# Attention on one Trainium2 core: the second head's softmax normalisation on GpSimd, with the delta masks queued behind it unit by unit

## The chip, the cores and the metric

One core of a Trainium2 chip runs the whole program. Five engines work side by side: TensorE (matrix products and transposes; PE in the profile, its weight loads PEld), VectorE (DVE), ScalarE (ACT), GpSimd (POOL) and SyncE (SP, which here issues the transfers). Each has its own queue of instructions, and they wait for one another through semaphores only. The metric is device time in microseconds (us), the median of several runs.

## The reference

The program is one layer of a hybrid encoder on 1024 + 512 tokens of width 1024, in float32. The part at issue is the neighbourhood attention: 8 heads of 64, tokens on a grid 64 wide, and for each block of 16 columns and 8 rows of queries the keys of some rows of 32 columns.

```python
s = jnp.einsum("bjqhd,bijkhd->bhjqik", q_r, k_r).astype(jnp.float32)
bias = rpb[:, dr_idx[None, None, :, None], dc_idx[:, :, None, :]]
s = jnp.where(col_ok[:, :, None, :], s + bias, -jnp.inf)
p = jax.nn.softmax(s.reshape(s.shape[:4] + (kh * NA_KB,)), axis=-1).reshape(s.shape)
return jnp.einsum("bhjqik,bijkhd->bjqhd", p.astype(v.dtype), v_r)
```

After it comes a gated delta rule in chunks (`_delta_rule_chunked`). It needs decay matrices `exp(g_i - g_j)` that are cut to the lower (or, for the backward direction, upper) triangle, with and without the diagonal, and a triangular solve, which the kernel does by joining blocks of doubling size.

## The kernel before

The program is a row of stages with a barrier of all engines between them: projection, attention, delta rule, merge, MLP. The change lies in `attention` (L994 to L1263) and its helper `delta_masks` (L1266 to L1293).

`attention` goes over 48 units `u`: 4 pairs of heads, in each 3 groups of 8 rows, in each 4 column blocks. A unit is two heads of 128 queries against 384 keys (units 0 to 7 of a pair) or 256 keys (units 8 to 11); this number is its width. Its two heads are `h = 0` and `h = 1`. A unit goes through these steps, each an instruction or a few, and the steps of neighbouring units overlap:

- TensorE multiplies queries by keys into `ps_s` (L1129, the score). Two scores may be ahead.
- VectorE adds the bias, negates, takes the row minimum (L1186, into `sc` and `nmax`), once per head.
- ScalarE takes the exponential with the row sum (L1243, into `pr` and `rsum`), once per head.
- VectorE inverts both sums (L1193, `rinv`) and multiplies each head by its column of them (L1198, `pn`, the normalisation).
- TensorE transposes `pn` of both heads into `ps_t` (L1171, the turn of the heads).
- ScalarE copies that to `pt` (L1253), TensorE multiplies by the values into `ps_o` (L1158, the mix), VectorE copies the result out (L1220).

In the first 8 units of a pair TensorE also transposes values (L1141, the value turn), which VectorE copies (L1206). All loops are written out by hand: in iteration `u` TensorE's order is score of `u + 1`, mix of `u - 2`, value turn of `u`, turn of the heads of `u - 1`. VectorE's is bias of `u`, reciprocal and normalisation of `u - 1`, value copy of `u`, output copy of `u - 2`. ScalarE's is exponentials of `u`, copies of `u - 1`, then one or two exponentials of the delta rule's decay (L1233). `sc`, `pr`, `pn` and `pt` hold two units each.

Work for the delta rule is done in this stage beside the attention. GpSimd alone makes the masks: `strict` and `incl` (8 instructions) and then `join`, seven levels of ten small instructions each, all in one chain (`delta_masks`), and after them twelve additions of a mask to the decay rows `gq` (L1109, 128 x 512, into `dd0`). VectorE does eight small instructions on decay columns (`decay_columns`, L978 to L985) in iteration 6. SyncE's queue issues the loads of queries, keys, values, bias tables and decay rows. `join` is read in the stage after.

Of the kernel before, what the change touches and what calls it, by code (L numbers as in the profile page):

```python
# [18 lines left out]
ALU = mybir.AluOpType  # L19
AX = mybir.AxisListType  # L20

P = 128
# [5 lines left out]
TB = 512  # L28
NTB = T // TB
# [10 lines left out]
NEG = -1e30  # L40

HEADS = 4
LEVELS = 7
# [950 lines left out]
def attention(nc, proj, v_mid, bias_t, o_t, ident, masks, dn_y, g_rows, cols, ahead, oz):  # L994

    U = NH_PAIR * NA_UNITS
# [22 lines left out]
    strict, incl, join = masks  # L1019
    y2, gq, kb, col2, ncol2, cx2 = ahead  # L1020
    dd0 = kb[:].rearrange("p (a j) n -> p a j n", j=4)
    DG_AT, DCOL_AT, DY_AT, DEXP_AT = 1, 6, (28, 32, 36), 8
    DEXP = 2 * 2 * NTB * 4

    with Space(nc, "na") as s:
        dg_in, dy_in, d_cols, d_colexp, d_masked, d_exp, d_chain = (s.sem(x) for x in (
            "dg_in", "dy_in", "d_cols", "d_colexp", "d_masked", "d_exp", "d_chain"))
        q_in, k_in, v_in = ([[s.sem(f"{x}{a}{b}") for b in range(2)] for a in range(2)] for x in ("q_in", "k_in", "v_in"))
        bias_in = [s.sem(f"bias_in{b}") for b in range(NBB)]
        stored = [s.sem(f"stored{b}") for b in range(2)]  # L1030
        scored, biased, exped, recip, normed, turned, copied, mixed, out_done, v_turned, v_copied, seen = (s.sem(x) for x in (
            "scored", "biased", "exped", "recip", "normed", "turned", "copied", "mixed", "out_done", "v_turned", "v_copied",
            "seen"))
        mask_chain, mask_work = s.sem("mask_chain"), s.sb("mask_work", [P])
        qt, kt, vt = s.sb("qt", [2, T]), s.sb("kt", [2, T]), s.sb("vt", [2, 2, 2, T // 2])
# [65 lines left out]

        @block.gpsimd
        def _(pool):
            delta_masks(pool, mask_chain, mask_work, *masks)
            pool.wait_ge(dg_in, 32)
            for n in range(2 * NTB):
                tg, d = divmod(n, 2)
                for q, mask in enumerate((strict, incl)):
                    pool.tensor_tensor(dd0[:, 2 * n + q], gq[:, 0, d, tg * TB:(tg + 1) * TB].rearrange("p (j n) -> p j n", n=P),  # L1109
                                       mask[:, d].unsqueeze(1).to_broadcast([P, 4, P]), ALU.add).then_inc(d_masked, 1)  # L1110

        @block.tensor
        def _(pe):
            def score(u):
                i, g, j, k0, n, width = unit(u)
                if g == 0:
                    if j == 0:
                        pe.wait_ge(q_in[0][i % 2], 16 * (i // 2) + 16)
                        pe.wait_ge(k_in[0][i % 2], 16 * (i // 2) + 16)
                elif j == 0 and g == 1:  # L1120
                    pe.wait_ge(q_in[1][i % 2], 16 * (i // 2) + 16)
                    pe.wait_ge(k_in[1][i % 2], 16 * (i // 2) + 16)
                if u >= 2:
                    pe.wait_ge(biased, 2 * u - 2)
                keys = kt[:, i % 2].rearrange("p (r c) -> p r c", c=GRID)
                q = qt[:, i % 2, (g * NA_BLOCKS + j) * P:(g * NA_BLOCKS + j + 1) * P]
                for h in range(2):
                    r = slice(64 * h, 64 * h + 64)
                    last = pe.matmul(ps_s[:, u % 2, h, 0:width].rearrange("p (r c) -> p r c", c=NA_COLS), q[r],  # L1129
                                     keys[r, k0:k0 + n, na_col0(j):na_col0(j) + NA_COLS], start=True, stop=True,  # L1130
                                     tile_position=(64 * h, 0))
                last.then_inc(scored, 1)

            def turn_values(u):
                i, k = group(u)
                j, rest = k % NA_BLOCKS, k // NA_BLOCKS
                pe.wait_ge(v_in[rest][i % 2], 32 * (i // 2) + 32)
                v = vt[:, i % 2, j % 3 != 0, j // 2]
                for t in range(3):
                    at = (3 * rest + t) * P  # L1140
                    last = pe.transpose(ps_o[:, u % 2, (t + 1) * P:(t + 2) * P], v[:, at:at + P], ident[:])  # L1141
                last.then_inc(v_turned, 1)
            score(0)
            for u in range(U + 2):
                if u + 1 < U:
                    score(u + 1)
                m = u - 2
                if m >= 0:
                    i, g, j, k0, n, width = unit(m)
                    pe.wait_ge(copied, 2 * m + 2)  # L1150
                    pe.wait_ge(v_copied, groups_to(m))
                    if m >= 2:
                        pe.wait_ge(out_done, m - 1)
                    tiles = width // P
                    for t in range(tiles):
                        for h in range(2):
                            r = slice(64 * h, 64 * h + 64)
                            last = pe.matmul(ps_o[r, m % 2, 0:P], vtm[:, j, k0 // 4 + t, r], pt[:, m % 2 * 2 + h, t * P:(t + 1) * P],  # L1158
                                             start=(t == 0), stop=(t == tiles - 1), tile_position=(0, 64 * h))
                    last.then_inc(mixed, 1)  # L1160
                if group(u) is not None:
                    turn_values(u)
                m = u - 1
                if 0 <= m < U:
                    width = unit(m)[-1]
                    for h in range(2):
                        pe.wait_ge(normed, 2 * m + h + 1)
                        if m:
                            pe.wait_ge(copied, 2 * (m - 1) + h + 1)
                        for t in range(width // P):  # L1170
                            last = pe.transpose(ps_t[:, h, t * P:(t + 1) * P], pn[:, m % 2 * 2 + h, t * P:(t + 1) * P], ident[:])  # L1171
                        last.then_inc(turned, 1)

        @block.vector
        def _(dve):
            for u in range(U + 2):
# [13 lines left out]
                if 0 <= m < U:  # L1190
                    width = unit(m)[-1]
                    dve.wait_ge(exped, 2 * m + 2)
                    dve.reciprocal(rinv[:, 2 * m:2 * m + 2], rsum[:, 2 * m:2 * m + 2]).then_inc(recip, 1)  # L1193
                    dve.wait_ge(recip, m + 1)
                    for h in range(2):
                        if m >= 2:
                            dve.wait_ge(turned, 2 * (m - 2) + h + 1)
                        dve.tensor_scalar(pn[:, m % 2 * 2 + h, 0:width], pr[:, m % 2 * 2 + h, 0:width],  # L1198
                                          rinv[:, 2 * m + h:2 * m + h + 1], None, ALU.mult).then_inc(normed, 1)
                if group(u) is not None:  # L1200
                    i, k = group(u)
                    j, rest = k % NA_BLOCKS, k // NA_BLOCKS
# [22 lines left out]
        def _(act):  # L1225
# [10 lines left out]
            for u in range(U + 1):  # L1236
                if u < U:
                    width = unit(u)[-1]
                    for h in range(2):
                        act.wait_ge(biased, 2 * u + h + 1)  # L1240
                        if u >= 2:
                            act.wait_ge(normed, 2 * (u - 2) + h + 1)
                        act.activation(pr[:, u % 2 * 2 + h, 0:width], sc[:, u % 2 * 2 + h, 0:width], ACT.Exp,  # L1243
                                       bias=nmax[:, 2 * u + h:2 * u + h + 1], scale=-1.0,
                                       accum_out=rsum[:, 2 * u + h:2 * u + h + 1]).then_inc(exped, 1)
# [17 lines left out]
            act.wait_ge(d_colexp, 1)  # L1263


def delta_masks(pool, chain, work, strict, incl, join):  # L1266

    def keep(n, tile, pattern, base, step, fill=0.0):

        pool.wait_ge(chain, n)  # L1270
        pool.affine_select(out=tile, in_=tile, compare_op=ALU.is_ge, fill=fill, base=base, pattern=pattern,
                           channel_multiplier=step).then_inc(chain, 1)

    n = 0
    for tile, fill, col, row, base in ((strict[:, 0], -NEG, -1, 1, -1), (strict[:, 1], -NEG, 1, -1, -1),
                                       (incl[:, 0], NEG, 1, -1, 0), (incl[:, 1], NEG, -1, 1, 0)):
        pool.memset(tile, 0.0).then_inc(chain, 1)
        keep(n + 1, tile, [[col, P]], base, row, fill)
        n += 2
    for v in range(LEVELS):  # L1280
        m = 2 ** v
        for d in range(2):

            blocks = work[:].rearrange("p (c two m) -> p c two m", two=2, m=m)[:, :, 1 - d]
            pool.wait_ge(chain, n)
            pool.memset(work[:], 0.0).then_inc(chain, 1)
            pool.wait_ge(chain, n + 1)
            pool.memset(blocks, 1.0).then_inc(chain, 1)
            keep(n + 2, blocks, [[-2 * m, P // (2 * m)], [0, m]], -d * m, 1)
            keep(n + 3, blocks, [[2 * m, P // (2 * m)], [0, m]], m - 1 + d * m, -1)  # L1290
            pool.wait_ge(chain, n + 4)
            pool.tensor_copy(join[:, v, d], work[:]).then_inc(chain, 1)
            n += 5  # L1293
    pool.wait_ge(chain, n)


DCHAINS = [(d, g) for g in range(len(SEG)) for d in range(2)]
# [1274 lines left out]
```

## Time and profile before

| | |
|---|---|
| median of 3 runs | 3128.47 us (3127.68 to 3128.94) |
| the profiled execution | 3127.74 us, its span 3126.0 us |
| mean granted clock of TensorE | 0.983 |
| busy in the span | PE 2993.6 us (96%), DVE 1334.8 (43%), ACT 1152.9 (37%), POOL 1184.4 (38%) |
| attention stage, 1100 to 1252 us | PE 128.3 us busy, DVE 116.6, ACT 106.8, POOL 36.7; clock 0.91 |
| L1198 in it | 96 instructions, 36.5 us |
| L1109 in it | 12 instructions of about 1.3 us |

The times are those of one profiled execution, counted from the start of its span. An instruction's time includes what it waits for once its engine has begun it. In brackets stands how long the engine was idle before an instruction, and which instruction, by the semaphores, ended that. PEclk is the share of full speed (2.4 GHz) that TensorE was granted; 0.50 is 1.2 GHz. The timeline merges neighbouring instructions of one kind: x2 is two of them, and the time is from the start of the first to the end of the last.

### The profile page before, as it was taken

To read this page: it belongs to the slowest core of one execution; us is meant where nothing else is said; L and a number is where in the kernel's file an instruction comes from. 1 tells how busy PE (TensorE), PEld (TensorE's weight loads), DVE (VectorE), ACT (ScalarE), POOL (GpSimd) and SP (SyncE) were. 2 spreads that over 40 slices of the span, in tenths; PEclk is the share of its full clock that TensorE was granted. 3 is DMA by queue.
4 is the path that set the end of the run, shared out by engine and by line. 5 is a ranking of instruction groups with operands and counts; after the bars stand their busy time and mean duration, and the time that the engine had idled before them with its cause. 6 is when DMAs were issued, how large, how long until landed. Compare 5 with 4: busy or idle time off the path is not lost. (4 is left out here: it accounts for less than half of the span.)

```text
span 3126.0 us, 44278 instructions
## 1 busy us (share of the span) xinstructions
PE 2993.6 (96%) x17907; PEld 2451.2 (78%) x17907; DVE 1334.8 (43%) x1933; ACT 1152.9 (37%) x1932; POOL 1184.4 (38%) x777
## 2 busy tenths in 40 slices
PE   5999999999999969899998999979999999999998
PEld 4878787877888746788887887868888888888887
DVE  4233232312379968667664353122224232322323
ACT  4241413243144548566664122232232323333222
POOL 4221121212123240123200433456665666666764
PEclk8999999999999989999999999989999999999999
DMA  4434232433545375111103545332333233333331
GB/s 112 164 137 131 75 117 83 134 102 118 164 143 175 112 245 185 64 53 56 39 22 112 175 148 170 95 125 91 108 92 97 89 100 122 94 95 95 109 114 61
DMA packets 239594, 353.15 MB, mean 113 GB/s; under 512 B 32928, under 2 KB 186272, under 8 KB 239392
## 3 DMA queue, kind: packets, MB, share of 16 engines
q1 hardware_dynamic: 239392, 350.32, 34.6%
q8 instruction: 144, 2.36, 0.3%
q14 instruction: 58, 0.48, 0.0%
HBM read 263.71 MB, written 96.36 MB: 115 GB/s over the span
## 5 line engine op out<-in xcount | busy, mean ns | idle before, releaser
L102 PE MATMUL pj_acc<-u_hi,pj_w_hi 128*128 128x512 f32 x1464 | 576.2, 394 | 13.0 <-POOL u_lo L543 13.0
L2484 DVE TENSOR_TENSOR x_tm<-m_ps,x_tm 128x512 f32<-128x512 f32 x384 | 265.0, 691 | 744.1 <-PE m_ps L104 744.1
L104 PE MATMUL pj_acc<-u_hi,pj_w_lo 128*128 128x512 f32 x1464 | 571.7, 390 | 0.0
L103 PE MATMUL pj_acc<-u_lo,pj_w_hi 128*128 128x512 f32 x1464 | 571.2, 390 | 0.0
L537 POOL TENSOR_TENSOR pj_w_lo<-pj_w_raw,pj_w_hi 128x1024 fp32r<-128x1024 f32 x61 | 157.8, 2586 | 729.7 <-ACT pj_w_hi L586 729.7
L102 PEld LDWEIGHTS pj_acc<-u_hi,pj_w_hi 128*128 128x128 f32 x1464 | 275.7, 188 | 88.0 <-issue 18.2
L2361 POOL TENSOR_TENSOR m_w_lo<-m_w_raw,m_w_hi 128x1024 fp32r<-128x1024 f32 x96 | 237.8, 2501 | 263.0 <-ACT m_w_hi L2275 263.0
L104 PEld LDWEIGHTS pj_acc<-u_hi,pj_w_lo 128*128 128x128 f32 x1464 | 275.7, 188 | 58.2
L103 PEld LDWEIGHTS pj_acc<-u_lo,pj_w_hi 128*128 128x128 f32 x1464 | 275.9, 188 | 56.4
L102 PE MATMUL m_ps<-m_v_hi,m_w_hi 128*128 128x512 f32 x768 | 299.6, 390 | 2.4 <-DVE m_v_lo L2452 2.4
L102 PE MATMUL m_ps<-m_w_hi,m_h_hi 128*128 128x512 f32 x768 | 299.6, 390 | 0.0
L104 PE MATMUL m_ps<-m_v_hi,m_w_lo 128*128 128x512 f32 x768 | 299.3, 390 | 0.0
L103 PE MATMUL m_ps<-m_v_lo,m_w_hi 128*128 128x512 f32 x768 | 299.2, 390 | 0.0
L104 PE MATMUL m_ps<-m_w_hi,m_h_lo 128*128 128x512 f32 x768 | 298.9, 389 | 0.0
L103 PE MATMUL m_ps<-m_w_lo,m_h_hi 128*128 128x512 f32 x768 | 298.8, 389 | 0.0
L2354 POOL TENSOR_TENSOR m_w_lo<-m_w_raw,m_w_hi 128x1024 fp32r<-128x1024 f32 x96 | 227.8, 2395 | 22.7 <-ACT m_w_hi L2268 22.7
L2060 POOL TENSOR_TENSOR mo_w_lo<-mo_w_raw,mo_w_hi 128x512 fp32r<-128x512 f32 x72 | 94.2, 1308 | 307.1 <-ACT mo_w_hi L2022 307.1
L586 ACT CAST pj_w_hi<-pj_w_raw 128x1024 fp32r<-128x1024 f32 x61 | 63.8, 1046 | 375.8 <-PE pj_acc L104 375.2
L2287 ACT CAST m_h_hi<-m_rel 128x512 fp32r<-128x512 f32 x96 | 59.6, 621 | 357.7 <-POOL m_rel L2367 357.7
L2275 ACT CAST m_w_hi<-m_w_raw 128x1024 fp32r<-128x1024 f32 x96 | 96.1, 1050 | 247.6 <-PE m_ps L104 247.6
L102 PEld LDWEIGHTS m_ps<-m_v_hi,m_w_hi 128*128 128x128 f32 x768 | 144.6, 188 | 32.8 <-DVE m_v_lo L2452 2.8
L104 PEld LDWEIGHTS m_ps<-m_v_hi,m_w_lo 128*128 128x128 f32 x768 | 144.5, 188 | 30.1
(283 smaller groups left out, 5278.7 us busy)
## 6 DMA issues: line engine op xcount, KB each, us to landing
m_w_raw<-in_w_mlp_dram SPq DMA_DIRECT2D x48, 1024.0 KB, 5.4
m_w_raw<-in_w_mlp_dram SPq DMA_DIRECT2D x96, 512.0 KB, 3.6
proj<-pj_stage SPq DMA_DIRECT2D x61, 768.0 KB, 3.5
pj_w_raw<-in_w_in_dram SPq DMA_DIRECT2D x61, 512.0 KB, 5.1
mo_gate<-proj SPq DMA_DIRECT2D x24, 768.0 KB, 4.4
mo_w_raw<-in_w_out_dram SPq DMA_DIRECT2D x48, 256.0 KB, 2.6
rpb_bias<-pj_shut SPq DMA_DIRECT2D x48, 192.0 KB, 3.0
rpb_bias<-rpb_near SPq DMA_DIRECT2D x24, 384.0 KB
```

The lines of the kernel that those rows point to most:

```text
L102: pe.matmul(out, w_hi, x_hi, start=first, stop=False)
L103: pe.matmul(out, w_hi, x_lo, start=False, stop=False)
L104: return pe.matmul(out, w_lo, x_hi, start=False, stop=last)
L537: pool.tensor_tensor(w_lo[:, n % 2], w_raw[:, n % 2], w_hi[:, n % 2].bitcast(F32), ALU.subtract).then_inc(lo_done, 1)
L586: act.copy(w_hi[:, n % 2], w_raw[:, n % 2]).then_inc(hi_done, 1)
L2060: pool.tensor_tensor(w_lo[:, sl % 2], w_raw[:, sl % 3], w_hi[:, sl % 2].bitcast(F32), ALU.subtract).then_inc(w_lo_done, 1)
L2275: act.copy(w2_hi[:, (2 * gg + j) % 4], w2_raw[:, j]).then_inc(w2_hi_done, 1)
L2287: act.copy(h_hi[:, m % 4], rel[:, j]).then_inc(hh_done, 1)
L2354: pool.tensor_tensor(w1_lo[:, m % 4], w1_raw[:, :, j * P:(j + 1) * P], w1_hi[:, m % 4].bitcast(F32), ALU.subtract).then_inc(w1_lo_done, 1)
L2361: pool.tensor_tensor(w2_lo[:, m % 4], w2_raw[:, j], w2_hi[:, m % 4].bitcast(F32), ALU.subtract).then_inc(w2_lo_done, 1)
L2484: dve.tensor_tensor(xt, ps2[:, q % 4], xt, ALU.add).then_inc(added, 1)
```

## The change

The multiply of head 1 goes from VectorE to GpSimd, with a semaphore `normed_b` of its own; TensorE's turn of head 1 and ScalarE's reuse of `pr` wait for it. GpSimd's queue is rearranged: first only `strict` and `incl`, then for each unit the multiply, behind which stands one addition of L1109 in units 5 to 16 and one level of `join` in units 20 to 26.

```diff
@@ GpSimd's queue in attention
-            delta_masks(pool, mask_chain, mask_work, *masks)
-            pool.wait_ge(dg_in, 32)
-            for n in range(2 * NTB):
+            def normal(m):
+                width = unit(m)[-1]
+                pool.wait_ge(recip, m + 1)
+                if m >= 2:
+                    pool.wait_ge(turned, 2 * (m - 2) + 2)
+                pool.tensor_scalar(pn[:, m % 2 * 2 + 1, 0:width], pr[:, m % 2 * 2 + 1, 0:width],
+                                   rinv[:, 2 * m + 1:2 * m + 2], None, ALU.mult).then_inc(normed_b, 1)
+            def masked(a):
+                n, q = divmod(a, 2)
                 tg, d = divmod(n, 2)
-                for q, mask in enumerate((strict, incl)):
-                    pool.tensor_tensor(dd0[:, 2 * n + q], gq[:, 0, d, tg * TB:(tg + 1) * TB].rearrange("p (j n) -> p j n", n=P),
-                                       mask[:, d].unsqueeze(1).to_broadcast([P, 4, P]), ALU.add).then_inc(d_masked, 1)
+                if a == 0:
+                    pool.wait_ge(dg_in, 32)
+                pool.tensor_tensor(dd0[:, a], gq[:, 0, d, tg * TB:(tg + 1) * TB].rearrange("p (j n) -> p j n", n=P),
+                                   (strict, incl)[q][:, d].unsqueeze(1).to_broadcast([P, 4, P]), ALU.add).then_inc(d_masked, 1)
+            delta_masks(pool, mask_chain, mask_work, *masks, 0)
+            for m in range(U):
+                normal(m)
+                a = m - DEXP_AT + 3
+                if 0 <= a < 2 * 2 * NTB:
+                    masked(a)
+                v = m - DEXP_AT - 2 * 2 * NTB
+                if 0 <= v < LEVELS:
+                    delta_masks(pool, mask_chain, mask_work, *masks, v + 1)
@@ TensorE
-                        pe.wait_ge(normed, 2 * m + h + 1)
+                        pe.wait_ge((normed, normed_b)[h], m + 1)
@@ VectorE
-                    for h in range(2):
-                        if m >= 2:
-                            dve.wait_ge(turned, 2 * (m - 2) + h + 1)
-                        dve.tensor_scalar(pn[:, m % 2 * 2 + h, 0:width], pr[:, m % 2 * 2 + h, 0:width],
-                                          rinv[:, 2 * m + h:2 * m + h + 1], None, ALU.mult).then_inc(normed, 1)
+                    if m >= 2:
+                        dve.wait_ge(turned, 2 * (m - 2) + 1)
+                    dve.tensor_scalar(pn[:, m % 2 * 2, 0:width], pr[:, m % 2 * 2, 0:width],
+                                      rinv[:, 2 * m:2 * m + 1], None, ALU.mult).then_inc(normed, 1)
@@ ScalarE
-                            act.wait_ge(normed, 2 * (u - 2) + h + 1)
+                            act.wait_ge((normed, normed_b)[h], u - 1)
@@ delta_masks: part 0 makes strict and incl, part v + 1 makes level v of join
-def delta_masks(pool, chain, work, strict, incl, join):
+def delta_masks(pool, chain, work, strict, incl, join, part):
```

Here `DEXP_AT` is 8, `NTB` 3, `LEVELS` 7 and `U` 48.

## Rows read from the trace of the kernel before

**Rows 1.** busy time in one 10 us stretch; after the time: busy us (instructions) per engine, PEclk, DMA

```profile
1170.00:1180.00 10.00, 10.00 (x96) 6.94 (x94) 9.36 (x37) 9.06 (x29) 0.00 (x0) 1.00 0.52 160
```

**Rows 2.** timeline of all engines, one 384-wide unit; columns: start us, us, engine, line

```profile
1167.02 0.92 PE L1129 MATMUL na_ps_s<-na_kt,na_qt 64*128 64x384 f32 x4
...
1167.87 0.88 PE L1158 MATMUL na_ps_o<-na_pt,na_vtm 128*64 128x128 f32 x12
...
1168.10 0.16 DVE L1193 RECIPROCAL na_rinv<-na_rsum 128x2 f32<-128x2 f32 x1
...
1168.29 0.75 DVE L1198 TENSOR_SCALAR na_pn<-na_pr,na_rinv 128x384 f32<-128x384 f32 x2
...
1168.67 0.55 PE L1141 MATMUL na_ps_o<-ident,na_vt 128*128 128x128 f32 x3
...
1169.06 0.82 PE L1171 MATMUL na_ps_t<-ident,na_pn 128*128 128x128 f32 x6
1169.26 0.56 DVE L1206 COPY na_vtm<-na_ps_o 128x384 f32<-128x384 f32 x1 [0.22 <-PE na_ps_o L1141]
...
1169.81 0.92 PE L1129 MATMUL na_ps_s<-na_kt,na_qt 64*128 64x384 f32 x4
```

**Rows 3.** timeline of the tensor engine, one 256-wide unit

```profile
1182.39 0.70 PE L1129 MATMUL na_ps_s<-na_kt,na_qt 64*128 64x256 f32 x4
...
1183.61 0.42 PEld L1171 LDWEIGHTS na_ps_t<-ident,na_pn 128*128 128x128 f32 x4 [0.17 <-DVE na_pn L1198]
...
1184.20 0.92 PE L1129 MATMUL na_ps_s<-na_kt,na_qt 64*128 64x384 f32 x4
```

**Rows 4.** timeline of VectorE and GpSimd, units 5 to 7

```profile
1128.59 1.26 POOL L1109 TENSOR_TENSOR dn_kb<-dn_gq,strict 128x512 f32<-128x512 f32 x1 [1.65 <-DMA dn_gq<-g_rows]
...
1130.86 1.77 DVE L1198 TENSOR_SCALAR na_pn<-na_pr,na_rinv 128x384 f32<-128x384 f32 x2
...
1131.03 1.39 POOL L1109 TENSOR_TENSOR dn_kb<-dn_gq,strict 128x512 f32<-128x512 f32 x1
...
1134.36 2.19 DVE L1198 TENSOR_SCALAR na_pn<-na_pr,na_rinv 128x384 f32<-128x384 f32 x2
...
1136.95 0.78 DVE L978 COPY dn_col<-cols 128x48 f32<-128x48 f32 x1
...
1142.85 0.29 DVE L1220 COPY oz<-na_ps_o 128x128 f32<-128x128 f32 x1
```

**Rows 5.** timeline of VectorE in the stage after, the same small instructions alone

```profile
1316.51 0.17 DVE L978 COPY dn_col<-cols 128x48 f32<-128x48 f32 x1
...
1317.21 0.16 DVE L985 COPY dn_cx<-dn_gq 128x12 f32<-128x12 f32 x1
```

**Rows 6.** timeline of VectorE, L1198 for units 6, 11, 30 and 35

```profile
1144.30 0.75 DVE L1198 TENSOR_SCALAR na_pn<-na_pr,na_rinv 128x384 f32<-128x384 f32 x2
...
1157.29 0.62 DVE L1198 TENSOR_SCALAR na_pn<-na_pr,na_rinv 128x256 f32<-128x256 f32 x2
...
1206.53 0.75 DVE L1198 TENSOR_SCALAR na_pn<-na_pr,na_rinv 128x384 f32<-128x384 f32 x2
...
1217.13 0.61 DVE L1198 TENSOR_SCALAR na_pn<-na_pr,na_rinv 128x256 f32<-128x256 f32 x2
```

**Rows 7.** busy time in a 2 us stretch, columns as in Rows 1

```profile
1146.00:1148.00 2.00, 2.00 (x12) 1.10 (x12) 1.22 (x7) 1.66 (x6) 0.00 (x0) 0.50 1.01 309
```

**Rows 8.** timeline of GpSimd: first and last instruction of the seven mask levels, a copy

```profile
1102.93 0.21 POOL L1286 MEMSET na_mask_work<- 128x128 f32 x1
...
1126.62 0.31 POOL L1292 CAST join<-na_mask_work 128x128 uint8<-128x128 f32 x1
...
1252.43 3.40 POOL L1425 COPY dn_tn<-ident 128x512 f32<-128x512 f32 x6 [108.60 <-POOLq L78]
```

**Rows 9.** timeline of VectorE, L1198 for units 20 and 27

```profile
1180.78 0.62 DVE L1198 TENSOR_SCALAR na_pn<-na_pr,na_rinv 128x256 f32<-128x256 f32 x2
...
1198.17 0.75 DVE L1198 TENSOR_SCALAR na_pn<-na_pr,na_rinv 128x384 f32<-128x384 f32 x2
```

More of the change, by code:

```diff
@@ L1030, in attention @@
         stored = [s.sem(f"stored{b}") for b in range(2)]
-        scored, biased, exped, recip, normed, turned, copied, mixed, out_done, v_turned, v_copied, seen = (s.sem(x) for x in (
-            "scored", "biased", "exped", "recip", "normed", "turned", "copied", "mixed", "out_done", "v_turned", "v_copied",
+        scored, biased, exped, recip, normed, normed_b, turned, copied, mixed, out_done, v_turned, v_copied, seen = (s.sem(x) for x in (
+            "scored", "biased", "exped", "recip", "normed", "normed_b", "turned", "copied", "mixed", "out_done", "v_turned", "v_copied",
             "seen"))
@@ L1272, in keep @@
                            channel_multiplier=step).then_inc(chain, 1)
[L1274 to L1293, printed above, removed]
+    if part == 0:
+        n = 0
+        for tile, fill, col, row, base in ((strict[:, 0], -NEG, -1, 1, -1), (strict[:, 1], -NEG, 1, -1, -1),
+                                           (incl[:, 0], NEG, 1, -1, 0), (incl[:, 1], NEG, -1, 1, 0)):
+            pool.memset(tile, 0.0).then_inc(chain, 1)
+            keep(n + 1, tile, [[col, P]], base, row, fill)
+            n += 2
+        pool.wait_ge(chain, n)
+        return
+    v = part - 1
+    n = 8 + 10 * v
+    m = 2 ** v
+    for d in range(2):
+        blocks = work[:].rearrange("p (c two m) -> p c two m", two=2, m=m)[:, :, 1 - d]
+        pool.wait_ge(chain, n)
+        pool.memset(work[:], 0.0).then_inc(chain, 1)
+        pool.wait_ge(chain, n + 1)
+        pool.memset(blocks, 1.0).then_inc(chain, 1)
+        keep(n + 2, blocks, [[-2 * m, P // (2 * m)], [0, m]], -d * m, 1)
+        keep(n + 3, blocks, [[2 * m, P // (2 * m)], [0, m]], m - 1 + d * m, -1)
+        pool.wait_ge(chain, n + 4)
+        pool.tensor_copy(join[:, v, d], work[:]).then_inc(chain, 1)
+        n += 5
     pool.wait_ge(chain, n)
```

## The prediction

> **What bounds the kernel now.** The table of the page comes first: TensorE carries the end of the whole program, VectorE is busy 43% of it and GpSimd 38%. The change touches one stage of some 150 us, so I read that stage alone. Its busy times in a settled stretch [rows 1] show three engines that all look full: TensorE 10.00 of 10, VectorE 9.36, ScalarE 9.06. GpSimd does nothing. The question is which of the three sets the pace, and the timeline of one unit answers it [rows 2]. TensorE takes four pieces in a fixed order: score 1167.02 to 1167.87 (0.85), mix to 1168.67 (0.80), value turn to 1169.06 (0.39), turn of the two heads to 1169.81 (0.75). Together that is 2.79 us, the whole period, with no piece late. VectorE has a wait in the same unit: 0.22 us in front of L1206, for TensorE's value turn. So TensorE paces, and VectorE, though 94% busy, is the one that waits. A unit of width 256 has the same shape [rows 3]: 1184.20 - 1182.39 = 1.81 us from score to score, and the turn begins after a wait of 0.17 us on L1198, short enough to be TensorE's ordinary cost of a wait. Time taken off VectorE is therefore worth nothing while the stage runs undisturbed.
>
> **Where it is disturbed.** Around units 5 to 7 GpSimd runs its twelve mask additions (L1109, 1.26 us each) back to back [rows 4]. VectorE's two normalisations of a unit then take 1.77 and 2.19 us where they take 0.75 [rows 2], and eight small instructions (L978 to L985), which in the next stage need 1317.21 + 0.16 - 1316.51 = 0.86 us [rows 5], stretch here from 1136.95 to about 1142.7 [rows 4]. VectorE and GpSimd take turns: each VectorE instruction waits for a whole addition. TensorE gets nothing for some 5 us, and its granted clock falls to 0.50 [rows 7], the 1.2 GHz level. From unit 6 to unit 11 the stage then takes 1157.29 - 1144.30 = 12.99 us, against 1217.13 - 1206.53 = 10.60 us for the same units two pairs later [rows 6].
>
> **Part 1: the second head's multiply.** 48 instructions leave VectorE, about 0.31 to 0.38 us each (half of 0.62 and 0.75). In the settled units that is worth 0, by the argument above; the cover is TensorE, and if TensorE were not the pace it would be up to 0.35 us a unit. What counts is when the second head is ready. Before, that is 0.04 + 0.75 = 0.79 us after the reciprocal ends (1168.26 to 1169.04) [rows 2]. TensorE starts that head's three turns about 0.3 us after it starts the first head's (a little under half of the 0.75 us), so hardly before 1169.25: a margin of 0.2 us. After, GpSimd sees the reciprocal about 0.10 us late (my estimate; VectorE itself needs 0.03), finds VectorE's first-head multiply under way, and multiplies. No GpSimd multiply by a column is in the trace. Bounds for 384 wide: a GpSimd copy of 512 columns takes 3.40 / 6 = 0.57 us [rows 8], so by width 0.43; an addition of two tensors of 512 takes 1.26 [rows 4], so by width 0.95. It has one tensor input like the copy, and a multiply more: I take 0.55 (0.42 at 256, bounds 0.28 and 0.63). For the meeting with VectorE: the addition that began 0.17 us after a multiply of VectorE took 1.39 instead of 1.26 [rows 4], 0.13 more. Ready at 0.10 + 0.13 + 0.55 = 0.78 us, the same as before. Cost 0; above 0.75 us for the multiply it begins to cost.
>
> The Trainium skill, SBUF — State Buffer, section "Who interferes with whom", says of the port pair that VectorE and GpSimd share that the one who comes second "fully blocks" for the other's whole instruction. By that rule the second head would be ready at 0.04 + 0.38 + 0.55, about 1.0 us, which just uses up the margin. The trace bears out the blocking where the addition comes first (1.77 and 2.19 us [rows 4]), but shows only 0.13 us where the multiply comes first.
>
> **Part 2: the additions spread out.** One addition follows the multiply of each of units 5 to 16. The first stall loses 1.77 - 0.75 = 1.0 us and the second 2.19 - 0.75 = 1.4 us; following TensorE's order through them, of these 2.4 us some 2.0 reach L1206 of unit 6. The eight small instructions meet the tail of one addition instead of five of them: about 0.3 + 0.9 + 0.4 us in place of the 5.9 us from 1136.95 to 1142.85 [rows 4], 4.3 us less. TensorE is then idle for under 2 us, so I expect the clock to stay up, and units 6 to 11 to take 10.6 us and not 13.0: 2.4 us. Gain 2.0 + 4.3 + 2.4 = 8.7 us; 6.3 if the clock falls all the same. Against it, behind the 256-wide units 8 to 11 GpSimd needs 0.23 + 0.42 + 1.26, about 1.9 us, in a period of 1.81: 0.5 us lost in all.
>
> **Part 3: the mask levels, which I think are what decides.** Before, the seven levels (70 small instructions) run from 1102.93 to 1126.93, 24.0 us [rows 8], while nobody waits for GpSimd. After, level v stands behind the multiply of unit 20 + v, and the multiply of the next unit stands behind the level. A level takes 24.0 / 7 = 3.4 us on average, but units come every 1.8 to 2.8 us. So from unit 20 to 27 GpSimd is the pace, and it never waits: reciprocal of unit 20 at 1180.75 [rows 9], + 0.23 + 0.42 for its multiply, + 24.0 of levels, + 3 x 0.42 + 3 x 0.55 for units 21 to 26, + 7 x 0.10 between them, + 0.55 for unit 27: 1209.6. Before, unit 27 is ready at 1198.17 + 0.75 = 1198.9 [rows 9], with 0.2 us in hand. So 10.5 us are lost. The double buffers hide none of it, for TensorE can't turn the second head of a unit before GpSimd has written it, and L1158 of that unit and L1220 wait behind. TensorE will have gaps of 1 to 3 us in these units; I add 0.5 for its clock.
>
> **The sum.** -8.7 + 0.5 + 10.5 + 0.5 = +2.8 us. The profiled execution took 3127.74 us (its span 3126.0), so 3130.5; the median of the runs lies 0.73 us above that execution: 3131.3 us.
>
> **Rivals.**
> - *The multiply costs as much as an addition* (0.95 and 0.63 us), or takes the port first. In the mask stretch that adds 4 x 0.4 + 4 x 0.21 = 2.4 us. In some 28 other units of width 384 the second head is late by about 0.2, of which half to all reaches the period: about 4 us. Total +9.2: 3137.7. For it: every GpSimd row with two tensors is slow. Against: this multiply has one.
> - *The clock falls in the mask stretch.* TensorE works 1.8 us in every 4 to 5. If it enters the 384-wide units 24 to 26 at 0.50, each takes over 5 us where GpSimd needs 3.6. Up to 3 x 1.5 = 4.5 us more: 3135.8. For it: the fall in [rows 7]. Against: that one followed 5 us of complete idleness.
> - *VectorE is the pace after all, and the kernel gets faster.* Then each of the 41 units outside the stretch gains about 0.35 us, 14 us: 3131.3 - 14 = 3117. It decides if the period of a 384-wide unit falls below 2.6 us. For it: 9.36 of 10 busy. Against: the wait of 0.22 us in every such unit.
> - *The change does little of this:* the levels' delay is partly taken up by work done ahead (one unit of 2.8 us at most), giving 3128.5.
>
> **How the numbers follow.** Forecast as summed 0.50; multiply or port dearer 0.17; clock 0.15; VectorE the pace 0.10; levels partly absorbed 0.08. The likeliest case's own range is 3126 to 3134. 0.2% is 6.3 us, about what a measurement of this kernel can tell from no change: below 3122.2 counts as faster, above 3134.7 as slower. Faster: the VectorE rival and a little of the forecast's low end, 0.12. Slower: the first two rivals less a part that falls short, 0.28. The same: 0.60. The range of 3122 to 3138 leaves out the VectorE rival and the high ends of the others.
>
> **What would show it.** L1198's row on VectorE halves to 48 with no instruction of 1.7 us or more. The gap in front of L1206 in settled units grows from 0.22 to about 0.6 at a period of 2.79: right; a period of 2.4: the VectorE rival. The eight small instructions end within 2 us. The new GpSimd multiply's mean shows 0.55 or 0.95. Between units 20 and 27 GpSimd is busy without a break and TensorE's longest waits name it; if the starts of L1198 for units 20 and 27 are about 28 us apart instead of 17.4, part 3 is right. The prediction fails if the levels delay nobody (then faster by 8 us) or the clock drops for most of the stretch.

## The result, and the profile after

The changed kernel takes 3142.45 us (median of 5 runs, 3141.49 to 3146.05) against 3128.94 us (5 runs, 3127.68 to 3130.84) of the kernel before, measured together: a ratio of 1.0046, 95% interval 1.0035 to 1.0058. It is slower by 13.5 us. The forecast was 3131.3 with a range of 3122 to 3138, and no change within 0.2% as the likeliest outcome. Neither holds: the measured time lies beyond the dear end of the range.

The profiled execution (span 3142.4) loses it all in the attention stage. From GpSimd's first instruction there to its first in the next stage the stage took 1252.43 - 1100.44 = 151.99 us before and 1269.49 - 1101.15 = 168.34 us after, 16.35 us more; everything else takes the same 2974 us.

The first view is that of the groups of instructions, in the stage of the changed kernel. Behind the bar stand busy us and mean ns of one, and then the idle time before.

```profile
L1110 POOL TENSOR_SCALAR na_pn<-na_pr,na_rinv 128x384 f32<-128x384 f32 x32 | 45.8, 1431 | 49.8 <-DVE na_rinv L1212 49.3
...
L1110 POOL TENSOR_SCALAR na_pn<-na_pr,na_rinv 128x256 f32<-128x256 f32 x16 | 16.7, 1044 | 10.6 <-DVE na_rinv L1212 10.2
...
L1119 POOL TENSOR_TENSOR dn_kb<-dn_gq,strict 128x512 f32<-128x512 f32 x6 | 7.6, 1266 | 0.0
...
L1216 DVE TENSOR_SCALAR na_pn<-na_pr,na_rinv 128x384 f32<-128x384 f32 x32 | 14.3, 448 | 1.1
```

L1110 is GpSimd's multiply: 1431 ns at 384 columns, 1044 ns at 256. The estimate was 550 and 420, its upper bounds 950 and 630. The addition next to it, with two tensors and 512 columns, takes 1266. So here a GpSimd instruction with one tensor and a column takes longer for 384 columns than one with two tensors for 512.

A settled stretch, all engines, to be held against [rows 2] (units 40 and 41):

```profile
1246.12 0.16 DVE L1212 RECIPROCAL na_rinv<-na_rsum 128x2 f32<-128x2 f32 x1
1246.32 0.42 DVE L1216 TENSOR_SCALAR na_pn<-na_pr,na_rinv 128x384 f32<-128x384 f32 x1
1246.38 1.47 POOL L1110 TENSOR_SCALAR na_pn<-na_pr,na_rinv 128x384 f32<-128x384 f32 x1 [1.86 <-DVE na_rinv L1212]
...
1247.29 0.56 DVE L1224 COPY na_vtm<-na_ps_o 128x384 f32<-128x384 f32 x1 [0.55 <-PE na_ps_o L1160]
...
1247.90 0.31 PEld L1190 LDWEIGHTS na_ps_t<-ident,na_pn 128*128 128x128 f32 x3 [0.56 <-POOL na_pn L1110]
...
1249.11 0.42 DVE L1216 TENSOR_SCALAR na_pn<-na_pr,na_rinv 128x384 f32<-128x384 f32 x1
...
1250.61 0.56 DVE L1224 COPY na_vtm<-na_ps_o 128x384 f32<-128x384 f32 x1 [1.09 <-PE na_ps_o L1160]
...
1252.43 0.42 DVE L1216 TENSOR_SCALAR na_pn<-na_pr,na_rinv 128x384 f32<-128x384 f32 x1
```

GpSimd begins 0.06 us after VectorE and is done at 1246.38 + 1.47 = 1247.85; TensorE, which had turned the first head, waits 0.56 us for that and goes on at 1247.90. VectorE's multiplies start at 1246.32, 1249.11 and 1252.43: periods of 2.79 and 3.32 us alternate, 3.06 on average where [rows 2] had 2.79. VectorE's wait before L1224 (the L1206 of before) is 0.55 and 1.09 us where it was 0.22. So VectorE did get free, and waits longer.

The waits of TensorE on GpSimd's multiply in the whole stage, with total us, count and the longest:

```profile
PEld na_ps_t L1190 <- POOL na_pn L1110: 21.1, 26, 3.3
...
PE na_ps_t L1190 <- POOL na_pn L1110: 14.6, 21, 3.1
```

None of these existed before. The mask levels, in GpSimd's timeline:

```profile
1179.04 1.08 POOL L1110 TENSOR_SCALAR na_pn<-na_pr,na_rinv 128x256 f32<-128x256 f32 x1 [0.94 <-DVE na_rinv L1212]
1180.07 0.20 POOL L1308 MEMSET na_mask_work<- 128x128 f32 x1
...
1184.28 0.29 POOL L1314 CAST join<-na_mask_work 128x128 uint8<-128x128 f32 x1
1184.67 0.93 POOL L1110 TENSOR_SCALAR na_pn<-na_pr,na_rinv 128x256 f32<-128x256 f32 x1
1185.54 0.20 POOL L1308 MEMSET na_mask_work<- 128x128 f32 x1
...
1197.72 1.25 POOL L1110 TENSOR_SCALAR na_pn<-na_pr,na_rinv 128x384 f32<-128x384 f32 x1
...
1210.02 0.29 POOL L1314 CAST join<-na_mask_work 128x128 uint8<-128x128 f32 x1
1210.41 1.25 POOL L1110 TENSOR_SCALAR na_pn<-na_pr,na_rinv 128x384 f32<-128x384 f32 x1
```

To be held against [rows 8, 9]: unit 20's multiply begins at 1179.04, level 0 stands behind it until 1184.57, and only then comes unit 21's multiply, although its reciprocal has long been there. GpSimd has no idle time until unit 27's multiply at 1210.41. From unit 20 to unit 27 it is 31.4 us by these starts; by VectorE's own, which is ahead of GpSimd here, it is 29.0 us, against 17.4 before by those of [rows 9]. The multiplies take 0.93 and 1.25 us here, where no multiply of VectorE runs beside them: that is their price alone. VectorE's copies and biases, which read PSUM, do run beside some of them and make no difference.

VectorE in units 5 to 7, to be held against [rows 4, 5]:

```profile
1136.85 0.54 DVE L978 COPY dn_col<-cols 128x48 f32<-128x48 f32 x1
...
1137.92 0.17 DVE L985 COPY dn_cx<-dn_gq 128x12 f32<-128x12 f32 x1
...
1141.56 1.10 DVE L1216 TENSOR_SCALAR na_pn<-na_pr,na_rinv 128x384 f32<-128x384 f32 x1
```

The eight small instructions (L978 to L985) end at 1138.09, after 1.24 us, where they took 5.75. But a new blocked multiply stands at 1141.56: 1.10 us instead of 0.42, for it met an addition of GpSimd's that was under way, and GpSimd's own multiply stood behind that addition:

```profile
1141.18 1.26 POOL L1119 TENSOR_TENSOR dn_kb<-dn_gq,incl 128x512 f32<-128x512 f32 x1
...
1142.42 1.34 POOL L1110 TENSOR_SCALAR na_pn<-na_pr,na_rinv 128x384 f32<-128x384 f32 x1
```

TensorE's granted clock, in three windows (the column before the last two):

```profile
1142.00:1144.00 2.00, 2.00 (x13) 1.26 (x14) 0.66 (x1) 1.47 (x5) 2.00 (x3) 0.50 0.97 286
...
1184.00:1188.00 4.00, 2.35 (x8) 0.95 (x10) 0.00 (x0) 1.63 (x6) 3.38 (x11) 0.70 0.63 164
...
1196.00:1200.00 4.00, 3.29 (x19) 2.23 (x16) 2.20 (x8) 1.40 (x6) 3.38 (x11) 0.50 1.04 393
```

It was at 0.50 again around units 7 and 8. In the stretch of the levels it fell to 0.70 with TensorE busy for 2.35 of 4 us, and to 0.50 later on.

### The profile page after: what moved, and what is told of

It is laid out like the page before. It is cut to its first block and busy times, and to the rows that moved or that the text cites. A ratio compares the mean times of both kernels' runs of the same rounds, so it can differ in the third digit from the quotient of the medians.

```text
span 3142.4 us, 44324 instructions
## 1 busy us (share of the span) xinstructions
PE 3004.4 (96%) x17907; PEld 2453.4 (78%) x17907; DVE 1316.0 (42%) x1885; ACT 1155.3 (37%) x1932; POOL 1244.8 (40%) x825
```

## The experiments

Where the stage's time goes, by the starts of VectorE's reciprocal (L1193 of before) in each kernel's timeline: us from the stage's start to unit 6, then from unit to unit, then the whole stage up to GpSimd's first instruction of the next. What follows unit 47 is 6.5 to 6.6 us in every kernel and has no column. Each row is one profiled execution.

| kernel | to 6 | 6 to 8 | 8 to 20 | 20 to 27 | 27 to 47 | stage | median of all runs |
|---|---|---|---|---|---|---|---|
| before | 43.66 | 5.85 | 30.63 | 17.40 | 47.91 | 151.99 | 3128.94; 3128.49; 3127.14 |
| changed | 38.33 | 6.31 | 33.00 | 29.01 | 55.13 | 168.34 | 3142.45 |
| e1 both on VectorE | 36.93 | 6.18 | 36.80 | 17.51 | 47.91 | 151.86 | 3129.18 |
| e2 levels in gaps | 39.91 | 4.78 | 33.25 | 18.81 | 53.01 | 156.30 | 3131.19 |
| e4 two-tensor multiply | 38.68 | 6.20 | 32.33 | 26.52 | 53.87 | 164.15 | 3138.63 |
| e5 no second multiply | 36.31 | 5.52 | 34.65 | 17.41 | 47.90 | 148.33 | 3124.17 |
| e6 last 128 columns | 38.92 | 4.06 | 29.98 | 17.44 | 47.95 | 144.90 | 3121.20 |
| e7 additions behind multiplies | 37.47 | 4.05 | 29.92 | 17.52 | 47.91 | 143.40 | 3119.67 |
| e8 two-tensor and gaps | 37.47 | 5.34 | 33.13 | 18.89 | 52.66 | 154.04 | 3128.51 |
| e9 before, paced additions | 36.92 | 4.05 | 29.88 | 17.41 | 47.91 | 142.71 | 3116.36 |

The three medians of before are those of the three sets in which it ran beside the changed kernel, e1 to e5, and e6 to e9. In the two later sets its runs spread over 3122 to 3133 us, more than in the first. What lies outside the stage, which no edit touches, takes between 2970.5 and 2978.2 us in the ten profiled executions (span less stage), while equal pieces of the stage agree within 0.12 us (the columns 20 to 27 and 27 to 47 of before, e1, e5, e7 and e9). So the stage's length is the sharper measure of one cause, and the ratio, with its interval, that of the whole.

**e1: both multiplies on VectorE, GpSimd's other work still spread.**

```diff
@@ GpSimd: the multiply goes, the wait for each unit stays
             def normal(m):
                 pool.wait_ge(recip, m + 1)
-                if m >= 2:
-                    pool.wait_ge(turned, 2 * (m - 2) + 2)
-                pool.tensor_scalar(pn[:, m % 2 * 2 + 1, 0:width], pr[:, m % 2 * 2 + 1, 0:width],
-                                   rinv[:, 2 * m + 1:2 * m + 2], None, ALU.mult).then_inc(normed_b, 1)
@@ VectorE
+                    if m >= 2:
+                        dve.wait_ge(turned, 2 * (m - 2) + 2)
+                    dve.tensor_scalar(pn[:, m % 2 * 2 + 1, 0:width], pr[:, m % 2 * 2 + 1, 0:width],
+                                      rinv[:, 2 * m + 1:2 * m + 2], None, ALU.mult).then_inc(normed_b, 1)
```

> Both multiplies stay on VectorE; GpSimd's additions and mask levels stay spread over the units as in the change (it still waits for each unit's reciprocal). Theory A (the loss is the GpSimd multiply, dear by itself and queued behind the levels; the spreading alone is a gain): the gaps of part 2 stay closed and nobody waits for the levels, 3128.9 - 8 = about 3121 us, and L1198's successor again takes 0.75 us for two. Rival B (the spread work on GpSimd itself disturbs VectorE in every unit through what the two share): no better than before, 3129 us or more, with VectorE's multiplies longer than 0.42 us in units 5 to 16 and 20 to 26.

Ratio to before 1.0001 (0.9992 to 1.0009): neither theory whole. The stretch of the levels is back at 17.51 us and the last one at 47.91, so the levels cost nothing with no multiply behind them. The closed gap is there too (36.93 to unit 6). But from unit 8 to 20 the stage loses 6.2 us. VectorE and GpSimd in units 13 and 14:

```profile
1160.55 1.53 DVE L1211 TENSOR_SCALAR na_pn<-na_pr,na_rinv 128x384 f32<-128x384 f32 x1
1160.59 1.27 POOL L1114 TENSOR_TENSOR dn_kb<-dn_gq,strict 128x512 f32<-128x512 f32 x1 [2.32 <-DVE na_rinv L1207]
...
1162.00 0.41 DVE L1215 TENSOR_SCALAR na_pn<-na_pr,na_rinv 128x384 f32<-128x384 f32 x1
...
1164.13 1.53 DVE L1211 TENSOR_SCALAR na_pn<-na_pr,na_rinv 128x384 f32<-128x384 f32 x1
1164.18 1.27 POOL L1114 TENSOR_TENSOR dn_kb<-dn_gq,incl 128x512 f32<-128x512 f32 x1 [2.32 <-DVE na_rinv L1207]
```

VectorE's first multiply begins at 1160.55, GpSimd's addition at 1160.59, both released by the same reciprocal, and the multiply takes 1.53 us: the addition has its 1.27 us undisturbed, and the multiply ends 0.22 us after it. That is the rival's mark, an instruction of 1.5 us in place of 0.42. It belongs to this kernel, in which the additions start together with VectorE's multiply; in the changed one GpSimd's own multiply stands in front of them.

**e2: the levels in GpSimd's idle time.** `delta_masks` is cut into half levels.

```diff
-                v = m - DEXP_AT - 2 * 2 * NTB
-                if 0 <= v < LEVELS:
-                    delta_masks(pool, mask_chain, mask_work, *masks, v + 1)
+                for x in LEVEL_AT.get(m, ()):
+                    delta_masks(pool, mask_chain, mask_work, *masks, x + 1)
@@ before the loop
+            LEVEL_AT = {-1: (0, 1, 2, 3), 2: (4, 5, 6, 7), 3: (8, 9), 4: (10,), 17: (11,), 24: (12,), 28: (13,)}
+            for x in LEVEL_AT[-1]:
+                delta_masks(pool, mask_chain, mask_work, *masks, x + 1)
```

> The change, but the fourteen half levels stand where GpSimd was idle in the changed kernel: four before unit 0, four behind unit 2, two behind unit 3, one each behind units 4, 17, 24 and 28. Theory A: units 20 to 27 took 31.4 us against 17.4 before; without the levels they take about 19 (the dear multiply stays), so 3142.5 - 12 = about 3130 us. Rival C (the levels are incidental, the clock of TensorE or the multiply alone makes the loss): over 3138 us.

Ratio 1.0011 (1.0002 to 1.0020). The stage is 12.0 us shorter than in the changed kernel, 10.2 of them between units 20 and 27 and 2.1 behind. That is close to theory A's number. What is left over before from unit 8 on is 53.01 against 47.91 us in the last twenty units, 1.4 between 20 and 27, 2.6 between 8 and 20. That the first two are the multiply on GpSimd is shown by e5 below, which has the same half levels and no such multiply, and is back at 47.90 and 17.41.

**e4: GpSimd's multiply as a product of two tensors.**

```diff
-                pool.tensor_scalar(pn[:, m % 2 * 2 + 1, 0:width], pr[:, m % 2 * 2 + 1, 0:width],
-                                   rinv[:, 2 * m + 1:2 * m + 2], None, ALU.mult).then_inc(normed_b, 1)
+                pool.tensor_tensor(pn[:, m % 2 * 2 + 1, 0:width], pr[:, m % 2 * 2 + 1, 0:width],
+                                   rinv[:, 2 * m + 1:2 * m + 2].to_broadcast([P, width]), ALU.mult).then_inc(normed_b, 1)
```

> The change, with GpSimd's multiply written as a product of two tensors, the column of reciprocals spread over the width. Theory A1 (the form with a scalar column is what makes 1.25 and 0.93 us alone): 0.95 and 0.63 us alone as the prediction's upper bound had it, 0.22 more beside VectorE, and the kernel about 3136 us. Rival A2 (the price is that of a multiply or of its columns in any form): 1.25 us or more again and 3142 us.

Ratio 1.0035 (1.0022 to 1.0049), 3138.6 us: between A1's 3136 and A2's 3142. The stage is 4.2 us shorter than the changed kernel's. The groups on GpSimd, then VectorE's first multiply beside GpSimd's in a settled unit:

```profile
L1110 POOL TENSOR_TENSOR na_pn<-na_pr,na_rinv 128x384 f32<-128x384 f32 x32 | 26.6, 831 | 64.6 <-DVE na_rinv L1212 64.2
...
L1110 POOL TENSOR_TENSOR na_pn<-na_pr,na_rinv 128x256 f32<-128x256 f32 x16 | 9.9, 620 | 16.1 <-DVE na_rinv L1212 15.9
```

```profile
1235.42 1.09 DVE L1216 TENSOR_SCALAR na_pn<-na_pr,na_rinv 128x384 f32<-128x384 f32 x1
1235.46 0.83 POOL L1110 TENSOR_TENSOR na_pn<-na_pr,na_rinv 128x384 f32<-128x384 f32 x1 [2.36 <-DVE na_rinv L1212]
```

The form was the price: 831 and 620 ns for the same products, less even than A1 had put it. And yet the period is only 3.0 us instead of 3.06, because now GpSimd takes its 0.83 us undisturbed and VectorE's multiply of the first head takes 1.09 instead of 0.42: the lateness moved from head 1 to head 0.

**e5: head 1 is not normalised** (TensorE turns `pr`, and ScalarE's reuse of `pr` waits for that turn; the output lacks the division), half levels as in e2.

```diff
-                        pe.wait_ge((normed, normed_b)[h], m + 1)
+                        pe.wait_ge((normed, recip)[h], m + 1)
@@ the source of each turn
-pn[:, m % 2 * 2 + h, t * P:(t + 1) * P]
+(pn, pr)[h][:, m % 2 * 2 + h, t * P:(t + 1) * P]
```

> Head 1 is not normalised at all: TensorE turns its exponentials straight from pr. GpSimd has no multiply, its half levels stand as in the run with the levels in gaps. Theory A (TensorE is the pace of a settled unit): VectorE does 0.38 us less a unit and the period of a 384-wide unit stays 2.79 us, the kernel within 3 us of the run with both multiplies on VectorE, about 3120 us. Rival D (VectorE is the pace): 2.4 us a unit and about 3107 us.

Ratio 0.9991 (0.9981 to 1.0000). A settled unit:

```profile
1224.68 0.30 PEld L1145 LDWEIGHTS na_ps_s<-na_kt,na_qt 64*128 64x128 f32 x4 [0.17 <-issue]
...
1226.91 0.56 DVE L1221 COPY na_vtm<-na_ps_o 128x384 f32<-128x384 f32 x1 [0.55 <-PE na_ps_o L1157]
...
1227.46 0.30 PEld L1145 LDWEIGHTS na_ps_s<-na_kt,na_qt 64*128 64x128 f32 x4 [0.17 <-issue]
```

1227.46 - 1224.68 = 2.78 us from score to score, the period of [rows 2], and VectorE's wait grew from 0.22 to 0.55. With a third of a microsecond less to do in each unit, units 20 to 47 take what they took before (17.41 and 47.90 us). TensorE is the pace, and VectorE is not. The kernel's time missed the expected 3120 by 4 us. Units 8 to 20 take 34.65 us, 4.7 more than in e7 below: the additions start together with VectorE's multiply, as in e1.

**e7: as e1, each addition behind VectorE's second multiply.**

```diff
                 if a == 0:
                     pool.wait_ge(dg_in, 32)
+                pool.wait_ge(normed_b, a + DEXP_AT - 2)
```

> As the run with both multiplies on VectorE, but each addition waits for VectorE's second multiply of its unit instead of for the reciprocal. In that run units 12 to 17 had a period of 3.59 us against 2.79, with VectorE's first multiply at 1.53 us beside an addition that began 0.04 us after it. Theory A (the additions are harmless unless they start together with a multiply): the period is 2.79 again, the gain of the closed gap is kept, about 3121 us. Rival B (an addition costs VectorE its 1.1 us wherever it stands in a unit): 3128 us or more.

Ratio 0.9975 (0.9965 to 0.9986), a gain of 7.8 us by the ratio. Units 8 to 20 take 29.92 us, the period there is 2.79. The collision cost 6.9 us in e1, and the only edit is where the additions begin: about 1.1 us after the reciprocal's start where it had been 0.23.

**e9: the kernel before with nothing but that wait.**

```diff
                 for q, mask in enumerate((strict, incl)):
+                    pool.wait_ge(normed, 2 * (2 * n + q + DEXP_AT - 2))
```

> The kernel before with one wait added: each of the twelve additions on GpSimd waits for both multiplies of its unit (5 to 16). Mask levels stay where they were, at the start. Theory A: like the run before it, about 3121 us; the levels' place is of no matter as long as no multiply is queued behind them. Rival (moving the levels away from the start is part of the gain, since they disturb units 0 to 3): this one is 1 us or more slower than the other.

Ratio 0.9967 (0.9955 to 0.9980), the best kernel here: its stage is 9.28 us shorter than before, 0.69 shorter than e7's. Moving the levels was no part of the gain. VectorE and GpSimd in units 5 to 7, the stretch of [rows 4]:

```profile
1134.21 0.75 DVE L1199 TENSOR_SCALAR na_pn<-na_pr,na_rinv 128x384 f32<-128x384 f32 x2
...
1135.14 1.27 POOL L1110 TENSOR_TENSOR dn_kb<-dn_gq,strict 128x512 f32<-128x512 f32 x1 [7.15 <-DVE na_pn L1199]
...
1136.99 0.17 DVE L985 COPY dn_cx<-dn_gq 128x12 f32<-128x12 f32 x1
...
1138.74 0.75 DVE L1199 TENSOR_SCALAR na_pn<-na_pr,na_rinv 128x384 f32<-128x384 f32 x2
...
1139.57 1.28 POOL L1110 TENSOR_TENSOR dn_kb<-dn_gq,incl 128x512 f32<-128x512 f32 x1 [3.16 <-DVE na_pn L1199]
```

The eight small instructions end at 1137.16, the two multiplies take 0.75 us together again, and the additions fall between them. The clock, in the stretch that had it at 0.50:

```profile
1138.00:1142.00 4.00, 2.78 (x26) 2.04 (x27) 3.93 (x18) 3.15 (x10) 1.50 (x2) 1.00 0.51 144
1142.00:1146.00 4.00, 4.00 (x39) 2.60 (x38) 3.42 (x16) 3.89 (x14) 2.53 (x3) 1.00 0.38 118
```

It stays at 1.00.

**e8: the change with both mendings** (e4's multiply and e2's placing of the levels).

> The change with both mendings: GpSimd's multiply as a product of two tensors (0.83 us alone) and the levels in GpSimd's idle time. Theory A (two separate losses that add): 3142.5 - 11.3 (levels) - 4 (form) = about 3127 us, no better than before, because a settled 384-wide unit still takes 3.0 us instead of 2.79. Rival (once the levels are away the multiply on GpSimd pays): below 3122 us.

Ratio 1.0002 (0.9993 to 1.0011). The losses add to within 2 us (168.34 - 12.04 - 4.19 = 152.1 us for the stage, 154.04 measured), and what is left equals the gain of the spreading: a mended form of this change is worth nothing.

**e6: GpSimd multiplies only the last 128 columns of head 1**, half levels as in e2.

```diff
-                pool.tensor_scalar(pn[:, m % 2 * 2 + 1, 0:width], pr[:, m % 2 * 2 + 1, 0:width],
+                pool.tensor_scalar(pn[:, m % 2 * 2 + 1, width - P:width], pr[:, m % 2 * 2 + 1, width - P:width],
@@ VectorE, after its multiply of head 0
+                    dve.tensor_scalar(pn[:, m % 2 * 2 + 1, 0:width - P], pr[:, m % 2 * 2 + 1, 0:width - P],
+                                      rinv[:, 2 * m + 1:2 * m + 2], None, ALU.mult)
@@ TensorE, before the last of head 1's turns
+                            if h and t == width // P - 1:
+                                pe.wait_ge(normed_b, m + 1)
```

> The change with levels in the gaps, GpSimd multiplying only the last 128 columns of head 1 and VectorE the rest. From 1.25 and 0.93 us alone at 384 and 256 columns a line gives 0.61 at 128, 0.83 beside VectorE. Theory A (the period grows by how late GpSimd is beyond a margin of about 0.2 us): ready in time, 2.79 us a unit, 3123 to 3126 us in all. Rival E (a GpSimd multiply disturbs VectorE's two whatever its width): 3.0 us or more a unit and 3130 us or more.

Ratio 0.9977 (0.9966 to 0.9988), 3121.2 us by the median, a little below the expected span. One of its seven runs took 6032.95 us, which nothing here explains; the six others lie between 3117.4 and 3122.7. A settled unit:

```profile
1225.26 0.42 DVE L1220 TENSOR_SCALAR na_pn<-na_pr,na_rinv 128x384 f32<-128x384 f32 x1
1225.32 0.88 POOL L1110 TENSOR_SCALAR na_pn<-na_pr,na_rinv 128x128 f32<-128x128 f32 x1 [1.90 <-DVE na_rinv L1216]
...
1225.59 0.46 DVE L1224 TENSOR_SCALAR na_pn<-na_pr,na_rinv 128x256 f32<-128x256 f32 x1
...
1226.22 0.56 DVE L1232 COPY na_vtm<-na_ps_o 128x384 f32<-128x384 f32 x1 [0.17 <-PE na_ps_o L1162]
```

GpSimd's 128 columns take 0.88 us beside two instructions of VectorE's (the line through 1.25 and 0.93 us gives 0.61 alone, an estimate; in unit 3, where it began after both of VectorE's had ended, it took 0.60). They are ready at 1226.20, and TensorE's turn runs through without a wait: 47.95 us for units 27 to 47. As soon as GpSimd is in time, its multiply costs nothing in these units, and gains nothing either (47.91 in e7 without it).

## Why the prediction was wrong

**What bounds: right.** TensorE paces the settled units; e5 takes away VectorE's work and the period stays 2.78 to 2.79.

**Part 1, the second head's multiply: the step that failed.** The prediction priced it "0.55 (0.42 at 256, bounds 0.28 and 0.63)" and at 384 bounded it by 0.43 and 0.95, from a copy and from an addition of two tensors. It measured 1.25 and 0.93 us alone and 1.47 and 1.08 beside VectorE, outside the bounds. The bound from above rested on the thought that an instruction with one tensor can't be dearer than one with two; e4 shows the opposite (0.83 and 0.62 for two). The mechanism was laid out rightly: the prediction said that "above 0.75 us for the multiply it begins to cost", and 1.47 us makes the period 3.06. No run tests the 0.75 itself: at 0.83 us (e4) it is the first head that comes late, and e6, at 0.88 us, has only the last third of the columns to deliver. The term was 0; it measured 2.6 + 1.4 + 5.1 = 9.1 us (e2 against before, from unit 8 on). The rival "the multiply costs as much as an addition" named this loss and was too cheap as well, at a surcharge of 6.4 us over the forecast; it set the dear end of the range, 3137.7.

**Part 2, the additions spread out: the place right, the size half.** To unit 6 the changed kernel gains 5.3 us, against 6.3 in the forecast; the eight small instructions end after 1.24 us. The 2.4 us of the clock did not come: it fell around units 7 and 8, as the prediction had allowed, after TensorE had waited first 1.4 us for VectorE's multiply of unit 6 and then 0.8 us for GpSimd's. The full forecast of 8.7 us is what the additions give once they meet no multiply: 8.6 us in e7, 9.3 in e9. The 0.5 us that the prediction put on the additions behind GpSimd's multiply were no underestimate: in the changed kernel units 12 to 20, which hold five of them, take 23.12 us, and units 36 to 44, which hold none, 23.12 as well. What it had no price for is an addition released together with VectorE's multiply, which holds that up for 1.1 us (e1, 6.2 us in all); the changed kernel is spared that by the multiply in front. [Rows 4] held a relative of it: the 1.77 us end at 1132.63, 0.21 after the addition of 1131.03 does. But not "each VectorE instruction waits for a whole addition": in the same trace the copy L1206 out of PSUM took 0.54 us at 1132.56, beside an addition from 1132.38 to 1133.76.

**Part 3, the mask levels: right.** 10.5 us and 0.5 for the clock were forecast; taking the levels away (e2) gives 12.0, and e1 shows that they cost nothing with no multiply behind them. By the prediction's sum unit 27's second head is ready 1209.56 - 1180.75 = 28.81 us after unit 20's reciprocal ends; it was 1211.66 - 1178.95 = 32.71. That is 3.9 us later, and the eight multiplies in that queue were 5.0 us dearer than forecast (one at 1.08 and three at 0.93 for 0.42, four at 1.25 for 0.55), so the levels themselves were not underpriced. e4 agrees: with multiplies cheaper by 0.3 to 0.5 us each the seven units take 26.52 us instead of 29.01.

**The sum.** Stage against stage: -5.3 to unit 6, +0.5 to unit 8, +2.4, +11.6, +7.2 to unit 47, together +16.3 us. By cause: the levels 12.0 (forecast 11.0), the multiply and its meetings from unit 8 on 9.1 (0.5 in all), the spreading up to unit 8 gives back 4.8 (8.7). Of the 13.5 us by which the stage missed the forecast, 8.6 are thus Part 1, 3.9 Part 2 and 1.0 Part 3. In e9, where the spreading meets nothing, the stage is at unit 8 3.7 us sooner than in the changed kernel (40.97 against 44.64 us), although no level is in the queue yet: that is the shortfall of Part 2, the clock's share in it. The waits of units 6 and 7 speak for the late multiplies as its cause; it was not tried apart. The median moved by 13.5 us only; the stage is that of one profiled execution, which took 3144.17 us, 16.4 more than that of before (3127.74).

**The rivals.** VectorE is not the pace: in the middle of a run of 384-wide units no kernel has a period under 2.78 us. The clock did fall in the mask stretch (0.70 from 1184 to 1188, 0.50 from 1196 to 1200), but it set no pace: GpSimd has no idle time up to unit 27's multiply, and its multiplies of units 24 to 27 start (1210.41 - 1197.72) / 3 = 4.2 us apart at either clock, one level and one multiply. Whether it cost something behind unit 27 was not tried. "Levels partly absorbed" did not occur.

**The meeting of the two multiplies.** The Trainium skill, SBUF — State Buffer, section "Who interferes with whom", has whichever of the two issues first, GpSimd or a VectorE instruction in a two-port mode, hold the shared pair and the other one fully blocked. The prediction weighed it and went by a delay of 0.13 us. Where VectorE's multiply was let through, that rule would delay GpSimd by 0.42 - 0.06 = 0.36 us; it was 0.22 (1.47 against 1.25), between the two. Where VectorE was held up (1.53 against 0.42 in e1) it waited for the whole addition, as by that rule, but the one that the records have starting first was the one that waited (below).

## What to carry to other kernels

Before work is moved off an engine, look for the engine that this one waits for: 94% busy with a wait of 0.22 us in every unit was not the pace, and its relief was worth nothing. A queue in order makes every late instruction pay for all that stands in front of it, so background work belongs where nothing timed is behind it, and on GpSimd where VectorE has no multiply within SBUF due. A single wait that shifted twelve additions by 0.9 us was worth 6.9 us of the stage (e7 against e1), and the same wait in the kernel before, where they had run back to back, 9.3. Price an operation that the trace doesn't hold with an upper bound wide enough for another form of it.

## What the hardware showed beyond that

- On GpSimd, multiplying 384 columns by a per-partition scalar took 1.25 us alone, by a column spread over the width as second tensor 0.83 us; at 256 columns 0.93 and 0.61.
- The same two engines starting almost together ended both ways. GpSimd's scalar multiply, recorded 0.06 us after VectorE's, let it pass (0.42 us) and took 0.22 us longer itself. Its two-tensor instructions, recorded 0.04 us after VectorE's, went first (0.83 and 1.27 us, undisturbed), and VectorE's took 1.09 and 1.53. The form alone does not decide it: in e8 the same two-tensor multiply, behind a mask level, began 0.11 us after VectorE's and let it pass, at 1.00 us instead of 0.83. Which it is between 0.04 and 0.06 us, the form or the start, was not tried.

```profile
1169.94 1.23 DVE L1218 TENSOR_SCALAR na_pn<-na_pr,na_rinv 128x384 f32<-128x384 f32 x1
1169.99 0.83 POOL L1110 TENSOR_TENSOR na_pn<-na_pr,na_rinv 128x384 f32<-128x384 f32 x1 [0.64 <-DVE na_rinv L1214]
...
1173.13 0.42 DVE L1218 TENSOR_SCALAR na_pn<-na_pr,na_rinv 128x384 f32<-128x384 f32 x1
1173.24 1.00 POOL L1110 TENSOR_TENSOR na_pn<-na_pr,na_rinv 128x384 f32<-128x384 f32 x1 [1.00 <-POOL join L1316]
```

- A GpSimd instruction follows a reciprocal of VectorE by 0.10 us (1246.28 to 1246.38), as estimated.
